# Attention layer of a two-layer backbone: the convolution unit of step 0 computed in two halves around the transposes

## The reference

```python
z = u_lat @ w_in                          # 1024 x 8192: B, C, X, G, Q, K, V, BG
y_a = z[B] * dwconv(z[C] * z[X], w_conv)  # short gated convolution
y_a = y_a * silu(z[G])
q, k, v = z[Q] * 64**-0.5, z[K], z[V]     # 16 heads of 64
y_b = neighbourhood_attention(q, k, v, k_ctx, v_ctx, rpb) * silu(z[BG])
y = concat(y_a, y_b) @ w_out
```

## Time and profile before

| | |
|---|---|
| median of 3 runs | 2388.96 us (2388.09 to 2391.47) |
| the profiled execution | 2387.58 us, of which 2385.8 us is the span of its instructions |
| TensorE busy in the span | 2257.1 us (95%) |
| VectorE, ScalarE, GpSimd busy | 1502.4 (63%), 1191.1 (50%), 510.0 us (21%) |
| TensorE clock granted, mean | 0.984 of full |
| the attention layer's pairs | from 102 us to 1270 us of the span |

### The profile page before, as it was taken

How to read it: one execution, slowest core, us unless ns; L and a number is a source line. 1 busy time by engine, 2 the same in 40 slices (tenths; PEclk the granted TensorE clock), 3 DMA queues, 4 the chain that set the end, 5 groups by cost and what they waited for, 6 DMA issues and landing times. The chain is left out here.

```text
span 2385.8 us, 33928 instructions
## 1 busy us (share of the span) xinstructions
PE 2257.1 (95%) x12000; PEld 1959.3 (82%) x12000; DVE 1502.4 (63%) x2381; ACT 1191.1 (50%) x1721; POOL 510.0 (21%) x296
## 2 busy tenths in 40 slices
PE   5999999999999999999997999799999999995998
PEld 3788888888888888888875888689898999894887
DVE  3576575765757658576586347557866786667444
ACT  4534434344343443434434234276787678767322
POOL 0132231322313223132220200112212221220300
PEclk9999999999999999999998999899999999997999
DMA  7111221112211122211107555111111111114654
GB/s 284 36 53 51 65 59 65 52 51 65 58 66 52 51 65 58 66 53 51 56 27 256 150 164 182 44 36 54 53 62 45 54 53 62 45 54 144 217 157 143
DMA packets 165414, 200.04 MB, mean 84 GB/s; under 512 B 51096, under 2 KB 125976, under 8 KB 162200
## 3 DMA queue, kind: packets, MB, share of 16 engines
q1 hardware_dynamic: 155336, 174.53, 23.5%
q10 hardware_dynamic: 9792, 23.07, 2.8%
q0 software_dynamic: 144, 0.52, 0.1%
HBM read 166.11 MB, written 31.98 MB: 83 GB/s over the span
## 5 line engine op out<-in xcount | busy, mean ns | idle before, releaser
L955 PE MATMUL ps<-u_hi,w_hi 128*128 128x512 f32 (+1 forms) x1464 | 532.9, 364 | 0.0
L955 PE MATMUL ps<-u_hi,w_lo 128*128 128x512 f32 (+1 forms) x1464 | 519.0, 355 | 0.0
L955 PE MATMUL ps<-u_lo,w_hi 128*128 128x512 f32 (+1 forms) x1464 | 517.7, 354 | 0.0
L955 PEld LDWEIGHTS ps<-u_hi,w_lo 128*128 128x128 f32 x1464 | 276.2, 189 | 39.9
L955 PEld LDWEIGHTS ps<-u_lo,w_hi 128*128 128x128 f32 x1464 | 277.0, 189 | 35.3
L955 PEld LDWEIGHTS ps<-u_hi,w_hi 128*128 128x128 f32 x1464 | 276.4, 189 | 35.3
L1633 POOL TENSOR_TENSOR o_w_lo<-o_w_raw,o_w_hi 128x1024 fp32r<-128x1024 f32 x48 | 138.9, 2895 | 670.6 <-ACT o_w_hi L1648 670.6
L1903 PE MATMUL ps<-u_hi,o_w_hi 128*128 128x426 f32 (+2 forms) x640 | 238.5, 373 | 14.0 <-POOL o_w_lo L1633 9.3
L573 ACT ACTIVATE probs<-probs,neg_max 128x640 f32<-128x640 f32 (+1 forms) x160 | 122.9, 768 | 249.9 <-DVE neg_max L776 248.8
L1903 PE MATMUL ps<-u_hi,o_w_lo 128*128 128x426 f32 (+2 forms) x640 | 237.8, 372 | 0.0
L1903 PE MATMUL ps<-u_lo,o_w_hi 128*128 128x426 f32 (+2 forms) x640 | 237.6, 371 | 0.0
(11 more groups left out here) (192 smaller groups left out, 4385.3 us busy)
## 6 DMA issues: line engine op xcount, KB each, us to landing
y_tile<-y_scratch SPq DMA_DIRECT2D x72, 512.0 KB, 5.0
w_stage<-in_w_even SPq DMA_DIRECT2D x63, 512.0 KB, 3.7
o_w_raw<-in_w_odd SPq DMA_DIRECT2D x48, 512.0 KB, 3.6
ada_piece<-in_w_ada SPq DMA_DIRECT2D x20, 1024.0 KB, 5.7
wout_raw<-in_w_out SPq DMA_DIRECT2D x16, 1024.0 KB, 9.7
y_scratch<-h_backward SPq DMA_DIRECT2D x16, 512.0 KB, 2.7
h_scratch<-h_tile ACTq DMA_DIRECT2D x18, 256.0 KB, 2.3
h_tile<-h_scratch ACTq DMA_DIRECT2D x18, 256.0 KB, 2.9
```

The lines of the kernel that those rows point to most:

```text
L955: last = nc.tensor.matmul(ps[:, bank(j, g), 0:t - f], w[:, slot, c * P:(c + 1) * P], x[:, c, f:t], start=(c == 0 and n == 0), stop=(c == K ...
```

## The change

At step 0 of each pair, the unit (CC, 0) is no longer computed whole behind the 5 transposes of `turn(i, 0)`, but its chunks 0 to 3 ahead of them and its chunks 4 to 7 behind. Nothing is added or removed: it is the same 24 matmuls and 5 transposes.

```diff
--- before.py
+++ after.py
@@ -1127,10 +1127,16 @@
                 for s in range(STEPS):
                     if s + 1 < STEPS:
                         scores(i, s + 1)
-                    turn(i, s)
+                    if s == 0:
+                        (j, g, c0, c1), = pieces(s, last)
+                        project(i, j, g, c0, KC // 2)
+                        turn(i, s)
+                        project(i, j, g, KC // 2, c1)
+                    else:
+                        turn(i, s)
                     if s == 14:
                         pe.wait_ge(row_done, i + 1)
-                    for j, g, c0, c1 in pieces(s, last):
+                    for j, g, c0, c1 in pieces(s, last) if s else []:
                         project(i, j, g, c0, c1)
                     if s == 0:
                         pe.wait_ge(st_lo, i * LO_PER + 5)
```

## The result

The changed kernel took 2396.84 us (median of 7 runs, 2392.56 to 2397.89) against 2388.24 us of the kernel before (7 runs, 2386.82 to 2392.23): ratio 1.003, 95% interval 1.0019 to 1.0041. That is 8.6 us slower, inside the range of the prediction, but more than twice its +3.8 us, and over the 0.2% up to which I had called "no difference" the likeliest outcome (0.73; I gave 0.24 to more). The profiled execution took 2395.01 us with a span of 2393.2, 7.4 us longer than the one before.

The account below looks back on a forecast made before the run. TensorE, 95% busy, was taken as the bound; its half unit would wait for bank 0 behind L783. Adding +0.48 us a pair, +3.8 us over eight pairs, to 2388.96 gave 2392.8 us, range 2390.0 to 2397.0.

Parts of the forecast that it names:

- the hole: TensorE's idle stretch between step 0's last scores and the transposes, waiting for VectorE's L783: about 1.05 us a pair.
- the chain behind the later transposes: ScalarE's and VectorE's work after step 0's transposes, 3.45 us later; L788 still 0.9 us early, step 1's L783 0.7.
- rival 1: L783 held by GpSimd's L480 delays step 1's transposes: 0.43 us a pair on top, 2396.3 us; chance 0.13.
- the sum: From 269.81 to the first `weigh` product: 6.25 us before, 6.73 after; +0.48 us a pair, +3.8 us over eight.
- first term: TensorE idle at step 0 from 269.81 until bank 0 is free and signalled at 270.41: 0.60 us a pair.
- Before the change the wait for the bank cost nothing, since the transposes hid it: At step 0, transposes began at 269.81 and the unit at 270.50, while bank 0 was free at 270.41.
- Rival 4: Bank 0's signal comes some tenths before L737's recorded end, warm transposes pay the rest: 0 to 2 us; chance 0.07.
- rival 2: Clock falls to 1.2 GHz behind TensorE's longer idle stretch each time: +5.6 us a pair, some 2437 us; chance 0.02.
- a granted clock under 1.00 in the pairs: Sign listed as showing the forecast wrong: TensorE's granted clock below full in the pairs.
- the 277.04 of the prediction's walk: Forecast end of step 1's L783, 0.40 us after GpSimd's L480; by the lock's rule 277.19; transposes due at 277.73.
- Rival 3: Bank 0 free when step 0's scores end, so the half fills the idle wait: -1.28 us a pair, 2378.7 us; chance 0.03.

Follow-up runs that it names:

- Experiment 1: Changed kernel with ScalarE's tanh of BG 1 ahead of step 0's exp and VectorE's gate L737 ahead of normalise: 2379.8 us, ratio 0.9958 to the kernel before.
- experiments 3, 4 and 8: Changed kernel with 2, 6 and all 8 chunks ahead of the transposes instead of 4: 2395.59, 2400.33 and 2414.97 us.
- experiment 2: Kernel before with only the earlier tanh and gate of BG 1, the unit whole behind the transposes: 2388.52 us, ratio 0.9997.
- experiment 4: Changed kernel with 6 chunks ahead of the transposes and 2 behind: 2400.33 us, ratio 1.0048 to the kernel before.

## Why the prediction was right and wrong

- **Right: what happens.** The half can't begin in the hole; the wait for `normed` gives way to one for bank 0 at L955, eight times, 1.58 us (1.48 forecast); five transposes behind running matmuls take 0.46 us; the chain behind the later transposes is covered, with 1.0 us to spare at `weigh` (0.9 forecast) and 1.07 us at step 1 (0.7 forecast). Experiment 1 shows the bank to be the cause by taking its wait away, experiments 3, 4 and 8 show the spare to be as large as read: enough for 2 and 4 chunks ahead, 0.5 us a pair short for 6, 1.8 for 8.
- **Luck: that 2396.84 lies inside the range.** The upper end, 2397.0, was put there for rival 1, the lock, which cost nothing; what filled the room was the part that goes with the idle stretch, which the sum had at nothing. Of the 8.6 us the sum explains little over half, with its first term put right.
- **Wrong: the step "Before the change the wait for the bank cost nothing, since the transposes hid it", and the 0.60 us built on it.** I gave VectorE's signal the 0.05 us that it takes behind L783. Behind L737 it is 0.15 us: L955 starts 0.83 us after L737's start in the changed kernel, and 0.82 before (269.68 to 270.50), where its own duration is 0.68. So the unit of the kernel before didn't start at 270.50 because the transposes took 0.69 us; it was held by the bank, and the transposes took 0.52 (experiment 2). The first term is 0.69, not 0.60, the sum +0.57 to +0.59 a pair, not +0.48: 4.7 us instead of 3.8. Rival 4 had the signal some tenths earlier than L737's recorded end; it came later.
- **Wrong: rival 2, the clock, with 0.02.** I argued from one window of 10 us that held 1.67 us of idle in all and kept its clock, and priced the fall as if it came in every pair. It comes in some: 5 pairs of 48, each 1.4 to 1.6 us, where I had said +5.6. The prediction named "a granted clock under 1.00 in the pairs" as a sign of being wrong: it is absent in the first profile and there in the three later ones of the same kernel. With the stretch filled the median goes down by 3.9 us. The one filled profile has no fall in its eight pairs, but at 5 falls in 48 pairs, two profiles in five would have none by chance. So the median speaks for filling as the cure, and the count alone doesn't. The Trainium skill, page "TensorE: Matmul & The Clock Gate", section "Why this matters for your kernels", asks to avoid idle gaps between bursts of matmuls, and has longer ones in mind than the 1.6 us here; the trace shows that shorter ones do it now and then.
- **The lock (rival 1)** cost nothing, as forecast. L783 of step 1 ran into GpSimd's L480 and took 0.93 us (276.86 to 277.79). In experiment 1 it began earlier, beside the tile before (L489), and took 1.08 us; with 6 chunks, where it started behind L480, it took 0.56. GpSimd in the changed kernel, and GpSimd and VectorE in experiment 1:

```profile
276.29 1.15 POOL L480 TENSOR_TENSOR bias_piece<-bias_piece,row_mask 128x576 f32<-128x576 f32 x1
```

```profile
272.11 2.18 POOL L489 TENSOR_TENSOR bias_tile<-bias_piece,col_mask 128x384 f32<-128x384 f32 x2
273.57 1.08 DVE L783 TENSOR_SCALAR probs<-probs,row_rcp 128x640 f32<-128x640 f32 x1
```

  The rule that the Trainium skill's page "SBUF — State Buffer" gives in "SBUF: two separate sides", that the second comer waits for the whole of the other's instruction, agrees with these traces in that L783 never ends before GpSimd's instruction. But it ends 0.35 us behind L480 (277.44) and 0.36 behind L489 (274.29), not its whole 0.55, which is the 277.04 of the prediction's walk rather than its 277.19.
- **Rival 3** was right as an if: with the bank free the half does fill the hole, 1.15 us a pair against the 1.28 that I gave it. The rest, 0.13, is about the 0.17 us of the transposes' 0.69 that was the bank's wait.

What stays open is where the clock's part lies. The falls seen in the pairs come to 5 in six profiles, 1.2 to 1.3 us an execution. The layer's end, where the clock falls for a time in every kernel, differs too. From the last pair's L1147 (L1153 with the change) to the first matmul of the output projection it is 22.6 us in the profile of before, and 24.1, 24.1, 24.3 and 25.2 in the four of the changed kernel. But it is 24.3 in the filled one and 24.1 in experiment 2 as well; and of the kernels with 2, 6 and 8 chunks ahead, which have the same wait for the bank, the first has 25.0 and the other two 22.7. So the longer end doesn't follow the idle stretch in these profiles, and whether the falls in the pairs have a part in it they don't say. Of the 8.6 us, 4.7 are shown to be the bank; about 4 go when the idle stretch is filled, by the medians, and little more than 1 of these 4 is seen in the pairs. Where the rest is saved is not shown.

## What to carry to other kernels

When work is moved ahead of a wait, look up every wait that the moved work brings along and where its signal stands in the other engine's queue: here it stood right behind the one to be filled, so the wait grew. The gain was one swap in that queue away, -9.4 us, and neither the swap nor the cut showed any gain alone. And when a row's duration ends at the start of the next instruction, ask what that instruction waited for before calling all of it the first one's cost.

## What the runs showed of the hardware that I had not expected

- After 1.6 us of idle TensorE between dense matmuls the granted clock fell to 0.50 in 5 of 48 pairs, and the matmuls behind it ran at 0.43 us from start to start instead of 0.23 for some 3 us, at a price of 1.4 to 1.6 us; after 0.9 us of idle, in the profiles of before and of experiment 2, in none of 16. Seven matmuls with an unread product in the stretch made the changed kernel 3.9 us faster.
- The matmul that waited started 0.15 us after the recorded end of L737, 0.10 after that of L788 (experiment 4) and 0.05 after that of L783. The first two read PSUM and the last only SBUF; whether that is the reason, or what TensorE has to load first, no run here shows.
